# A hybrid retention and sliding-window block on one core: w_out computed by quarters, the MLP's norm weight multiplied into w_up

## Reference

```python
hn = rms_norm(h, mix_norm_g)
proj = hn @ w_in                                # 6656 columns, split into rq, rk, rv, rg, sq, sk, sv, gr, gs
y_ret = rms_norm(retention(rq, rk, rv), ret_norm_g) * silu(rg)
y_swa = sliding_window_attention(sq, sk, sv)    # 16 heads of 64, window 128, sinks
merged = sigmoid(gr) * (y_ret @ w_ret_branch) + sigmoid(gs) * (y_swa @ w_swa_branch)
h = h + merged @ w_out                          # w_out 1024 x 1024
hn = rms_norm(h, mlp_norm_g)
h = h + square(relu(hn @ w_up)) @ w_down        # w_up 1024 x 4096, w_down 4096 x 1024
```

## Time and profile before

| | us |
|---|---|
| median of three runs | 1606.87 (1605.84 to 1606.91) |
| the profiled execution, its own time | 1606.59 |
| its span in the trace | 1604.8 |
| PE busy | 1594.5 (99% of the span) |
| DVE busy | 1061.9 (66%) |
| ACT busy | 780.8 (49%) |
| POOL busy | 420.5 (26%) |

### The profile page before, as it was taken

How to read it: one execution, slowest core, us unless ns; L and a number is a source line. 1 busy time by engine, 2 the same in 40 slices (tenths; PEclk the granted TensorE clock), 3 DMA queues, 4 the chain that set the end, 5 groups by cost and what they waited for, 6 DMA issues and landing times.

```text
span 1604.8 us, 22764 instructions
## 1 busy us (share of the span) xinstructions
PE 1594.5 (99%) x7942; PEld 1333.5 (83%) x7942; DVE 1061.9 (66%) x2064; ACT 780.8 (49%) x1605; POOL 420.5 (26%) x604
## 2 busy tenths in 40 slices
PE   9999999999999999999999999999999999999999
PEld 7888888889888888888888788888888888888887
DVE  7984656677757777776555348866656557756675
ACT  6633343455656767672122136655555454444442
POOL 0101010122348898864211000111122222100000
PEclk9999999999999999999999999999999999999999
DMA  8423232276445666568452122444444299633452
GB/s 298 183 99 119 97 123 84 92 251 242 143 138 154 166 175 166 159 159 268 157 191 92 66 90 108 145 164 145 145 154 164 113 326 354 233 97 95 153 181 92
DMA packets 130833, 255.95 MB, mean 159 GB/s; under 512 B 15024, under 2 KB 52320, under 8 KB 130720
## 3 DMA queue, kind: packets, MB, share of 16 engines
q1 hardware_dynamic: 85424, 130.64, 26.0%
q0 software_dynamic: 45008, 123.72, 23.0%
q10 hardware_dynamic: 288, 0.14, 0.0%
HBM read 159.67 MB, written 69.47 MB: 143 GB/s over the span
## 4 chain that ended last, share of the span: by engine, by line
PE 94%; DVE 3%; DMA 1%; ACT 1%; POOL 1%; issue 0%; DVEq 0%; ACTq 0%
PE bank L1222 29%; PE bank L1226 29%; PE bank L1227 29%; PE bank L1538 2%; PE bank L1570 1%; PE bank L1552 1%; DMA PW<-PR 1%; DVE WL L2436 1%; PE bank L1587 0%; PE bank L1265 0%; PE bank L1670 0%; PE bank L1620 0%; POOL PR L1097 0%; PE bank L1439 0%; PE bank L1574 0%
## 5 line engine op out<-in xcount | busy, mean ns | idle before, releaser
L1226 PE MATMUL bank<-WH,ADL 128*128 128x512 f32 x448 | 174.3, 389 | 0.0
L1222 PE MATMUL bank<-WH,ADH 128*128 128x512 f32 x448 | 174.3, 389 | 0.0
L1227 PE MATMUL bank<-WL,ADH 128*128 128x512 f32 x448 | 174.3, 389 | 0.0
L2362 ACT CAST ADH<-ARAW 128x512 fp32r<-128x512 f32 x112 | 69.7, 622 | 170.4 <-PE bank L1227 160.5
L1097 POOL TENSOR_SCALAR PR<-PR,RC 128x272 f32<-128x272 f32 (+1 forms) x128 | 138.3, 1215 | 48.2 <-DVE RC L2991 48.1
L3245 DVE TENSOR_TENSOR ADL<-ARAW,ADH 128x512 fp32r<-128x512 f32 x112 | 77.6, 692 | 96.7 <-ACT ADH L2362 96.5
L1222 PE MATMUL bank<-HN,WH 128*128 128x512 f32 x344 | 137.3, 399 | 0.1
L1226 PE MATMUL bank<-HN,WL 128*128 128x512 f32 x344 | 134.7, 392 | 0.0
L1227 PE MATMUL bank<-HN,WH 128*128 128x512 f32 x344 | 134.6, 391 | 0.0
L1222 PE MATMUL bank<-SOPH,WH 128*128 128x512 f32 x256 | 99.8, 390 | 0.0
L1226 PE MATMUL bank<-SOPH,WL 128*128 128x512 f32 x256 | 99.6, 389 | 0.0
(11 more groups left out here) (387 smaller groups left out, 4364.0 us busy)
## 6 DMA issues: line engine op xcount, KB each, us to landing
ARAW<-uop SPq DMA_DIRECT2D x112, 256.0 KB, 3.2
uop<-US POOLq DMA_DIRECT2D x64, 256.0 KB, 3.1
WRAW<-in_w_up SPq DMA_DIRECT2D x15, 1024.0 KB, 6.3
PW<-PR SPq DMA_DIRECT2D x56, 272.0 KB, 3.0
uop<-UA POOLq DMA_DIRECT2D x48, 256.0 KB, 3.2
RAW<-in_w_in SPq DMA_DIRECT2D x46, 256.0 KB, 3.9
gates<-TB POOLq DMA_DIRECT2D x40, 256.0 KB, 2.7
proj<-SA POOLq DMA_DIRECT2D x36, 256.0 KB, 2.3
```

What stands on the lines that cost most here:

```text
L1222: mm = pe.matmul(bank, ahi, bhi, start=first, stop=False, skip_group_check=onto)
L1226: pe.matmul(bank, alo, bhi, start=False, stop=False, skip_group_check=onto)
L1227: return pe.matmul(bank, ahi, blo, start=False, stop=last, skip_group_check=onto)
L2362: act.copy(ADH[:, n % 4, :], ARAW[:, n % 4, :]).then_inc(da_hi, 1)
```

## The change

**w_out by quarters.** `merged @ w_out` is now computed as 7 products on quarters of 512 x 512, in the order t = 0, 1, 2, 3, 5, 4, 6, each as 4 blocks f of 4 products k: 7 x 4 x 4 x 3 = 336 matmuls. Products 2, 4, 5 and 6 add onto what a bank holds. Sums of quarters of `merged` are made in the branch steps 20 to 31 (`op_sum`, `op_lo`, `op_hi`), sums of quarters of w_out behind them (`add_right` to `sum_all`, 20 on DVE). Of the four quarters SP loads the first (OPX) as before; OPR (1 MB) behind DVE's last gate multiplication, OPY (1 MB) behind the last branch matmul, OPZ in four pieces behind these. DVE has 28 evictions (`rest`) in place of 16.

**Rows.** Of x, POOL loads rows 2 to 7 for H1 only when the operands of step 28 are done (they came between the loads of gates before), 6 x 512 KB. Rows come in the order 0 to 7. `norm_h` is split: DVE inverts (`invert_h`), ACT scales the row (`scale_h`). Row 7 is transposed behind product (1,0).

**Norm weight.** GBM is gone; g stands as GCM, 128 x 8, one value for each row of w_up. POOL multiplies the w_up columns of f = 0, 1 and 2 with it (`scale_raw`, 8 instructions of 128x256, twice, and 16 of 128x128), ACT those of the others (`scale_up`, 8 instructions of 128x256 for each f), where before the weights were used as loaded.

**Order around it.** DVE's and ACT's streams around the last rows are written out anew, and the products of f = 0, 1, 2 use other PSUM banks.

```diff
+OSEQ = (0, 1, 2, 3, 5, 4, 6)
+OUT_ORDER = [(t, f) for t in OSEQ[:5] for f in range(4)] \
+    + [(4, 0), (4, 1), (6, 0), (4, 2), (6, 1), (4, 3), (6, 2), (6, 3)]
+ROWS_AT = {(5, 2): 0, (4, 0): 1, (4, 1): 2, (4, 2): 3, (6, 1): 4, (6, 2): 5, (6, 3): 6}
+ROWS_UP = {(1, 0): 7}
...
+            sp.wait_ge(d_free, DVE_F)
+            sp.dma_start(OPR[:, :, :], out_quarter(1, 0)).then_inc(opr_full, 16)
+            sp.wait_ge(d_full, DVE_F)
+            sp.dma_start(OPY[:, :, :], out_quarter(0, 1)).then_inc(opy_full, 16)
+            for k in range(4):
+                sp.wait_ge(raw_full[k], raw_count(SLAB_F, k))
+                sp.dma_start(OPZ[:, k, :], w_out[SL + k * P:SL + (k + 1) * P, SL:D]).then_inc(raw_full[k], 16)
...
-            for p, b in enumerate(ORD):
-                pool.wait_ge(xn_rdy, XN_ALL + p + 1)
+            pool.wait_ge(mg_rdy, MG0 + 28)
+            for b in range(2, NB):
+                load_rest(b)
...
+            def scale_raw(f, t, cols):
+                pool.wait_ge(uraw[f % 2], up_loaded(f, t))
+                for k in range(KT):
+                    part = WRAW[f % 2][:, k, cols]
+                    scaled = pool.tensor_scalar(part, part, GCM[:, k:k + 1], None, ALU.mult)
+                scaled.then_inc(pn_rdy, 1)
+            for b in range(4):
+                store_row(b)
+            pool.wait_ge(gm_full, 32)
+            scale_raw(0, 0, slice(0, 2 * P))
+            store_row(4)
+            store_row(5)
+            scale_raw(1, 0, slice(0, 2 * P))
+            store_row(6)
+            store_row(7)
+            scale_raw(2, 0, slice(0, P))
+            scale_raw(2, 2, slice(P, 2 * P))
...
+            for t, f in OUT_ORDER:
+                out_block(t, f)
+                if (t, f) in ROWS_AT:
+                    transpose_h(ROWS_AT[t, f])
...
-                    pe.wait_ge(hop_rdy, (17, 18, 18, 19, 20)[t - 2])
+                    pe.wait_ge(hop_rdy, (15, 15, 17, 19, 20)[t - 2])
...
+            def scale_h(p):
...
+                act.wait_ge(rstd_rdy, NB + 1 + p + 1)
+                if p:
+                    act.wait_ge(xt_full, XT_ALL + 2 * p)
+                for cols in (slice(0, SL), slice(SL, D)) if p == NB - 1 else (slice(0, D),):
+                    act.activation(ST[:, cols], H1[:, b, cols], ACT.Copy, scale=RSTD2[:, b:b + 1]).then_inc(xn_rdy, 1)
...
-                act.wait_ge(uraw[f % 2], up_loaded(f, t))
+                act.wait_ge(*up_scaled(f, t))
...
+                if 1 <= f < UF - 2 and t in (2, 4):
+                    scale_up(f + 2, range(4) if t == 2 else range(4, KT))
...
-                dve.scalar_tensor_tensor(out=ST[:, cols], in0=H1[:, b, cols], scalar=RSTD2[:, b:b + 1],
-                                         in1=GBM[:, cols], op0=ALU.mult, op1=ALU.mult).then_inc(xn_rdy, 1)
...
+            def rest(t, f):
+                b, c = (f + 4 if t in (3, 4, 6) else f), 0 if t in (0, 1, 6) else 1
...
+                dve.scalar_tensor_tensor(out=H1[:, b, cols], in0=out_bank(t, f)[:, :], scalar=-0.5 if t in (2, 4) else 0.5,
+                                         in1=H1[:, b, cols], op0=ALU.mult, op1=ALU.add).then_inc(d_free, 1)
...
+            rest(4, 3)
+            sum_2(4)
+            first_up_sums()
+            sum_4(4)
+            up_lo(0)
+            up_lo(1)
+            rest(6, 2)
+            lo_a22(4)
+            invert_h(6)
+            free_row(1)
...
+            lo_sums((5, 0), (5, 1), (5, 2))
+            up_lo(4)
+            sum_1(6)
+            up_lo(5)
+            sum_3(6)
+            lo_a22(6)
```

More of the change, by code:

```diff
@@ L2351, in _, with scale_up @@
             take_r1(0)
-            for q in range(6, WS):
-                up_hi(q)
+            hop_hi_first(7)
+            for b, i in SUM_SEQ[10:14]:
+                hi_sum(b, i)
+            up_hi(WS)
+            for b, i in SUM_SEQ[14:]:
+                hi_sum(b, i)
+            hi_a22(7)
+            def scale_up(f, ks):
+                act.wait_ge(uraw[f % 2], up_loaded(f, 0))
+                for k in ks:
+                    scaled = act.activation(WRAW[f % 2][:, k, :], WRAW[f % 2][:, k, :], ACT.Copy, scale=GCM[:, k:k + 1])
+                scaled.then_inc(e_rdy, 1)
             def down_hi(t, k):
@@ new lines, in _ @@
+            for k in range(4):
+                op_lo(5, k)
+            out_low(1)
+            for k in range(4):
+                add_right(k)
+            sum_three(0)
+            sum_three(1)
+            out_lo(2, 0)
+            sum_three(2)
+            out_lo(2, 1)
+            sum_three(3)
+            out_lo(2, 2)
+            out_lo(2, 3)
+            for f in range(4):
+                rest(0, f)
+            out_low(3)
+            for k in range(4):
+                add_corner(k)
@@ new lines, in _, with hop @@
+            for f in range(4):
+                rest(1, f)
+            for k in range(4):
+                sum_right(k)
+            for f in range(2):
+                rest(2, f)
+            for k in range(4):
+                sum_all(k)
+            for f in range(2, 4):
+                rest(2, f)
+            out_low(5)
+            for f in range(4):
+                rest(3, f)
+            out_low(4)
+            def hop(p):
+                hop_first(p)
+                hop_second(p)
+            rest(5, 0)
@@ new lines, in _ @@
+            invert_h(0)
+            rest(5, 1)
+            invert_h(1)
+            rest(5, 2)
+            rest(5, 3)
+            hop(0)
+            rest(4, 0)
+            out_low(6)
+            invert_h(2)
+            rest(4, 1)
+            hop(1)
+            invert_h(3)
+            rest(6, 0)
+            hop(2)
+            rest(4, 2)
+            invert_h(4)
+            rest(6, 1)
+            hop(3)
+            sum_1(4)
+            invert_h(5)
+            sum_3(4)
+            rest(4, 3)
@@ new lines, in _ @@
+            sum_2(4)
[7 more added lines that the diff above has]
+            free_row(1)
+            lo_sums((4, 0), (4, 1), (4, 2))
+            rest(6, 3)
+            sum_1(5)
+            invert_h(7)
+            sum_3(5)
+            up_lo(2)
+            sum_2(5)
+            up_lo(3)
+            sum_4(5)
+            lo_a22(5)
+            lo_sums((4, 3))
+            free_row(5)
@@ L3318, in _ @@
                 for one in up_new(q):
-                    up_lo(one)
+                    if one > WS:
+                        up_lo(one)
                 if f == UF - 1 and t in EARLY:
```

422 lines of the change are left out of this document (266 added, 156 removed).

## The result

Seven runs of each kernel: 1610.76 us median after (1610.55 to 1612.12), 1606.30 before (1605.73 to 1607.66). The ratio is 1.003, 95% interval 1.002 to 1.0041: 4.5 us slower. The profiled execution took 1610.66, its span is 1608.7, against 1606.59 and 1604.8 before.

The account below looks back on a forecast made before the run. PE, busy for 99% of the span, was taken to bound the kernel. To (0,4), -10.9 us of matmuls and waits of 12.8 for 1.8 gave +0.2; with +0.4 and +1.1, +1.7 on 1606.6: 1608, range 1600 to 1616.

Parts of the forecast that it names:

- A: The forecast itself: the chain from row to row swallows the matmul gain; 1608 us, own range 1604 to 1612, chance 0.50.
- Weights of w_out: Loads of w_out's quarters ahead of product 2: OPZ there at about 914.3, +0.4 us, bounds 0 and +6.4.
- Rival D: w_out's quarters OPY and OPZ land 3 to 6 us later behind H1's loads, product 2 waits: 1612 us, chance 0.18.
- Evictions and weight sums: On DVE: 12 more evictions and 20 sums, less eight norm multiplications, +10 to +13 us, beside PE's work until about 958.
- Row 2 and row 6: PE's waits ahead of these rows' transposes: 0.9 us behind ACT's casts of row 1, 3.3 behind row 6's late eviction.
- POOL: Scaling for (2,0) behind row 7's store: starts at 987, done at 993.6 (991.5 to 998.5), row 6's first sum at 996.3.
- (2,0): This MLP product waits 4.9 us until row 6's bank is read, and starts at 1000.05.
- (0,4): This MLP product waits 2.9 us for R2T, copied behind rows 6 and 7's casts; starts at 1013.85 instead of 1013.64.
- Behind (0,4): Later in the MLP, POOL's and ACT's scaling ahead of copies out of PSUM: waits of about 0.6 and 0.5, +1.1 us.
- rival B: PE keeps its gain, as waits at row 6, (2,0) and (0,4) shrink to 1 or 2 us: 1597 or 1601, chance 0.20.
- Rival C: DVE's two-input subtractions wait out POOL's scaling instructions on the shared port, 10 us at most: 1616 us, chance 0.12.
- M: Rival theory from the experiments: DVE and ACT are full from row 4 on, so a removed wait comes back elsewhere.

Follow-up runs that it names:

- e1: The changed kernel without POOL's 32 scaling instructions of w_up (f = 0, 1, 2): 1606.30 us.
- e2: The changed kernel with POOL's scaling of the first half of f = 2 ahead of the stores of rows 6 and 7: 1606.80 us.
- e11: The changed kernel without ACT's scaling of w_up (f = 3 to 15), POOL's kept: 1609.91 us.
- e4: The kernel before, with 48 of w_out's 384 matmuls left out and nothing added: 1600.27 us.
- e10: e9 without row 6's earlier eviction and norm, and with ACT's scaling of f = 3 where the change has it: 1608.24 us.
- e9: e7 with DVE's subtraction that completes R3T for (0,6) ahead of the first sums and subtractions for f = 1's weights: 1607.40 us.
- e12: e9 without POOL's 32 scaling instructions of w_up (f = 0, 1, 2): 1605.05 us.
- e6: The changed kernel with POOL's scaling ahead of the two stores, the first f's R2T and R3T copies earlier, and row 6's eviction and norm earlier: 1606.65 us.
- e7: e6 with ACT's first scaling of f = 3 behind the copy R3T of f = 1 instead of ahead of it: 1606.71 us.

## Why the prediction held, and what it had mis-sized

The time, 1610.8, lies in the range, 2.7 above the forecast of 1608 (+4.5 us in the median, +3.9 between the spans, where +1.7 was forecast). By the prediction's own line of 0.2% that is slower, to which it gave less (0.34) than to no change (0.45). The spans differ by 2.2 us more than forecast: 1.6 of it had come by (0,4), 1.0 came behind it, and 0.4 that was taken for w_out's weights did not come. The 1.8 us that the sum called waits before the change were a remainder: the trace has one wait of 0.7, and small gaps. The mechanism was A, the chain swallows the gain, step by step:

- *Branch steps*: no wait of PE there; 0.65 at the end, 0.8 forecast.
- *Weights of w_out*: +0.4 forecast, 0 measured. OPZ's pieces landed 7.9 to 8.4 us after their issue at 899.7 to 901.2, so by 909.6, not 914.3, and PE had no wait ahead of product 2. Rival D did not happen. Its load, by its tile (durations of the issue in ns, first and last issue):

```profile
L979 SPq DMA_DIRECT2D OPZ<-in_w_out x4: 430/430/504, 899.7 to 901.2; - x4
...
DMA to landing us min/median/max: 7.9/8.1/8.4
```

- *Evictions and weight sums*: +10 to +13 us forecast for DVE, +23.8 measured in S (70.26 to 94.05). The sum left out 15 more subtractions for w_out's weights (27 in place of 12) and 9 instructions of the last branch steps. PE did not wait for them: the growth lies ahead of 950, where PE was busy throughout. Windows as in the earlier trace rows, two of the kernel before, then two of the changed kernel:

```profile
895.69:950.00 54.31, 53.60 (x235) 43.74 (x234) 16.49 (x26) 10.80 (x17) 0.53 (x1) 1.00 0.25 83
950.00:1013.64 63.64, 63.64 (x312) 52.51 (x310) 53.77 (x84) 38.95 (x77) 4.27 (x8) 1.00 0.25 92
...
895.60:950.00 54.40, 54.40 (x244) 45.13 (x245) 45.84 (x76) 22.94 (x38) 4.21 (x8) 1.00 0.34 126
950.00:1015.47 65.47, 55.85 (x255) 45.39 (x253) 48.22 (x80) 45.90 (x85) 28.02 (x31) 0.92 0.29 97
```

- *Row 2 and row 6*: 0.9 and 3.7, forecast 0.9 and 3.3. Row 6's transposes began at 982.31, forecast 982.5.
- *POOL*: ready at 994.86, forecast 993.6 (991.5 to 998.5), since the eight instructions took 7.65 us, not 6.6. This is the term that was most too small. Row 6's first sum at 997.65, forecast 996.3. e1 and e2 confirm the link: without it, or with it earlier, (2,0) has no wait.
- *(2,0)*: it began at 1000.25, forecast 1000.05. That this agrees is luck: s, row 6's first sum, was 1.35 late, but (2,0) followed it by 2.6 us, not by 3.75. The wait was 2.6 in place of 4.9, since PE got there 2.4 later, by eight matmuls (1.8) and row 6's transposes (0.8) at the slow clock.
- *(0,4)*: the wait was 2.4, forecast 2.9; it began at 1015.47, forecast 1013.85. s was 1.3 late, and R2T 0.3 more.
- *Behind (0,4)*: +2.1, forecast 1.1. The wait ahead of (1,5) was 1.0, forecast 0.5; the rest are small gaps between 1029 and 1051. No matmul there ran at the slow clock, and behind 1060 PE was busy throughout.
- *ACT's scaling from f = 4 on*: hidden, as forecast (e11).

**A term that was missing is the clock, though it is not what made the sum too small.** Waits were priced by their length. In the wait of 3.7 us the granted clock fell to 1.2 GHz, and again behind the one of 2.6, and 15 matmuls took 3.1 us more. Eight of them lie ahead of the wait for (2,0), seven ahead of the wait for (0,4). Both waits end with the chain behind POOL's scaling, on DVE and ACT, so at the full clock PE would have waited longer by about as much. That is argued from the trace; no run holds the clock fixed. Where no wait follows the slow matmuls, their price stays: in e2 the twelve behind (0,4) took 2.6 us more, and the tail is 2.7 longer than before.

**One argument of it fell.** That R2T's copy ended 0.06 us ahead of (0,4) was read as a chain without slack. e4 shows that the old chain moves along with PE: 48 matmuls fewer, and (0,4) began 6.9 us sooner after w_out's start, without a wait of its own, with R2T's copy again 0.07 ahead of it. So the copy could come sooner, and its closeness to its use was no measure of slack. The sum did not rest on it, but on the added work; e4's 1600.3 lies where rival B had put a change that costs nothing (1597 to 1601).

**Rival C** (DVE waits out POOL) didn't hold: beside POOL, DVE's subtractions took up to 0.90 in place of 0.68, while POOL took 7.65 for eight instructions, of which the shortest lasted 0.59 and the longest 1.43. DVE's timeline there:

```profile
987.34 0.90 DVE L3430 TENSOR_TENSOR WL<-WRAW,WH 128x512 fp32r<-128x512 f32 x1 [1.31 <-ACT WH L2469]
...
990.67 0.75 DVE L3377 TENSOR_TENSOR SOPL<-RA,SOPH 128x512 fp32r<-128x512 f32 x1
991.35 0.68 DVE L3377 TENSOR_TENSOR SOPL<-S1B,SOPH 128x512 fp32r<-128x512 f32 x1
991.95 0.77 DVE L3377 TENSOR_TENSOR SOPL<-RA,SOPH 128x512 fp32r<-128x512 f32 x1
```

All of POOL's scaling (min/median/max ns, first and last start):

```profile
L1272 POOL TENSOR_SCALAR WRAW<-WRAW,GCM x32: 592/916/1781, 964.1 to 1024.8; 128x256 f32<-128x256 f32 x16, 128x128 f32<-128x128 f32 x16
```

By the rule of the Trainium skill (page "SBUF — State Buffer", section "Who interferes with whom") the one that comes second is blocked fully. The trace agrees only for POOL: POOL lost most, and DVE 0.1 to 0.2 us an instruction, less than any of POOL's lasts.

**What the experiments add to the prediction.** It priced the loss as waits at single places. e2 to e10 say more: only POOL's order gave time back (4.0 us by the medians; S + tail 713.1 to 709.9). After it, three more waits were taken away, one at a time, and S + tail stayed within 708.9 to 709.9, since S shrank and the tail grew. That speaks for M: from row 4 to f = 2 the streams of DVE, ACT and POOL hold work whose order is a chain, and removing PE's wait for one link uncovers the next. It is the order more than the amount: from 950 to (0,4) DVE is busy for 48.2 of 65.5 us, less than before (53.8 of 63.6), and ACT for 45.9. POOL's scaling is one link of it (e9 to e12: 2.4 by the medians). e12's 706.2 is still 4.0 above e4's 702.2, with PE's work the same; by the medians it is 4.8. What these are is open. The 12 more evictions, the 20 weight sums and the new order of rows are left to account for them, but no run took these away, and most of that work lies ahead of 950, where PE had no wait. No version that left nothing out was faster than the kernel before; e2, e6 and e7 can't be told from it.

## What to carry to other kernels

Work taken from a busy engine is worth only what the chains beside it leave, and how close an operand lands to its use doesn't tell how much that is. A cheap test is to leave the same work out of the old kernel and add nothing (here 5.4 to 6.9 of 10.9 us arrived), before the code that makes it possible is written. When a wait is moved, add up the whole stretch and its tail; one wait less is not yet time gained.

## Not expected of the hardware

Behind a wait, PE can lose time beyond the wait's length: at the granted clock of 1.2 GHz matmuls started 0.43 us apart in place of 0.23. In the changed kernel 15 of them in S took 3.1 us more beside 9.6 of waits, and the waits behind them took that up; in e2, twelve with no wait behind them made the tail 2.6 us longer. In e12, with waits of up to 2.6, none ran at that clock; in e9, behind waits of 1.9 and 3.8, 15 did.
